# A four-block transformer-like network on one core: the high and low parts of x in one 512-column matmul in the gated feed-forwards

## The reference, cut to what matters

```python
D_MODEL, SEQ, D_FF = 1024, 256, 2816

def _rms_norm(x, g):
    y = x * lax.rsqrt(jnp.mean(x * x, axis=-1, keepdims=True) + 1e-6)
    return y * g

def _swiglu(x, w_gu, w_down):            # w_gu: 1024 x 5632, w_down: 2816 x 1024
    g, u = jnp.split(x @ w_gu, 2, axis=-1)
    return (jax.nn.silu(g) * u) @ w_down

# in each of the 4 layers, before and after the mixer:
x = x + 0.5 * _swiglu(_rms_norm(x, ffn_norm), w_gu, w_down)
```

## Time and profile before

| | us |
|---|---|
| median of 3 runs | 2880.78 (2880.45 to 2882.35) |
| profiled execution, its span (first to last instruction) | 2880.3 |
| TensorE matmul busy | 2797.6 (97%) |
| TensorE weight loads busy | 2594.2 (90%) |
| VectorE busy | 1953.6 (68%) |
| ScalarE busy | 1438.5 (50%) |
| HBM traffic | 478.46 MB, 166 GB/s |

### The profile page before, as it was taken

The page is one execution under the profiler, slowest core; times in us unless marked ns, Lnnn a source line. Parts: engine busy times, 40 slices in busy tenths (PEclk is TensorE's granted clock), DMA queues, the critical chain, the costliest instruction groups (busy, mean ns, idle before and its releaser), DMA issues.

```text
span 2880.3 us, 48145 instructions
## 1 busy us (share of the span) xinstructions
PE 2797.6 (97%) x20356; PEld 2594.2 (90%) x20356; DVE 1953.6 (68%) x2547; ACT 1438.5 (50%) x1970; POOL 94.6 (3%) x147
## 2 busy tenths in 40 slices
PE   8999989999999999999999999999899999999998
PEld 8999869999997999998889999988799989988997
DVE  5757876565666656556655565588755788767877
ACT  5445554444456444445544444456444644455543
POOL 0000000000012000001100000000000100000000
PEclk9999999999999999999999999999999999999999
DMA  7654336575552655553345555443465456544563
GB/s 245 205 162 146 125 113 202 184 211 188 163 163 73 213 190 177 189 176 93 108 140 188 176 190 185 153 147 111 140 196 184 152 176 211 179 161 139 174 215 102
DMA packets 406282, 478.46 MB, mean 166 GB/s; under 512 B 16634, under 2 KB 332820, under 8 KB 406068
## 3 DMA queue, kind: packets, MB, share of 16 engines
q1 hardware_dynamic: 404244, 469.07, 50.7%
q0 software_dynamic: 1632, 6.25, 0.8%
q10 hardware_dynamic: 192, 0.08, 0.0%
HBM read 474.29 MB, written 1.05 MB: 165 GB/s over the span
## 4 chain that ended last, share of the span: by engine, by line
PE 88%; DVE 7%; ACT 3%; issue 2%; POOL 0%; DMA 0%; ACTq 0%; POOLq 0%; DVEq 0%
PE Wk L710 18%; PE Wk L712 18%; PE Wk L711 18%; PE Y L710 10%; PE Y L711 9%; PE Y L712 9%; DVE w_lo L2006 2%; DVE work L2306 1%; PE Wk L1090 1%; PE Y L819 1%; ACT w_hi L1431 1%; PE Y L1103 1%; PE Y L1000 1%; PE Y L1074 0%; ACT work L1726 0%
## 5 line engine op out<-in xcount | busy, mean ns | idle before, releaser
L2006 DVE TENSOR_TENSOR w_lo<-ring,w_hi 128x1024 fp32r<-128x1024 f32 (+2 forms) x910 | 1068.2, 1199 | 561.6 <-ACT w_hi L1431 517.7
L710 PE MATMUL Wk<-xT_hi,w_hi 128*128 128x256 f32 x4320 | 1230.0, 285 | 7.5 <-DVE w_lo L2006 3.5
L712 PE MATMUL Wk<-xT_hi,w_lo 128*128 128x256 f32 x4320 | 1222.3, 283 | 0.0
L711 PE MATMUL Wk<-xT_lo,w_hi 128*128 128x256 f32 x4320 | 1222.2, 283 | 0.0
L1431 ACT ACTIVATE w_hi<-ring 128x1024 fp32r<-128x1024 f32 (+1 forms) x894 | 907.1, 1039 | 597.2 <-PE Wk L712 420.5
L710 PEld LDWEIGHTS Wk<-xT_hi,w_hi 128*128 128x128 f32 x4320 | 828.3, 192 | 18.7 <-issue 7.6
L711 PEld LDWEIGHTS Wk<-xT_lo,w_hi 128*128 128x128 f32 x4320 | 828.5, 192 | 4.7 <-issue 1.0
L712 PEld LDWEIGHTS Wk<-xT_hi,w_lo 128*128 128x128 f32 x4320 | 828.4, 192 | 0.0
L710 PE MATMUL Y<-w_hi,hid_hi 128*128 128x512 f32 x936 | 368.6, 394 | 5.0 <-issue 3.0
L711 PE MATMUL Y<-w_lo,hid_hi 128*128 128x512 f32 x936 | 365.8, 391 | 0.0
L712 PE MATMUL Y<-w_hi,hid_lo 128*128 128x512 f32 x936 | 364.4, 389 | 0.0
(11 more groups left out here) (308 smaller groups left out, 2661.0 us busy)
## 6 DMA issues: line engine op xcount, KB each, us to landing
ring<-in_ffn_w_gu SPq DMA_DIRECT2D x352, 512.0 KB, 4.4
ring<-in_ffn_w_down SPq DMA_DIRECT2D x224, 512.0 KB, 4.1
ring<-in_ffn_w_up SPq DMA_DIRECT2D x96, 512.0 KB, 6.3
ring<-in_hg_w_in SPq DMA_DIRECT2D x80, 512.0 KB, 3.6
ring<-in_na_w_in SPq DMA_DIRECT2D x24, 512.0 KB, 4.0
ring<-in_hg_w_out SPq DMA_DIRECT2D x16, 512.0 KB, 3.2
ring<-in_lru_w_in SPq DMA_DIRECT2D x16, 512.0 KB, 3.8
ring<-in_kv_w SPq DMA_DIRECT2D x16, 512.0 KB, 5.1
```

The lines of the kernel that those rows point to most:

```text
L710: pe.matmul(o, l_hi, r_hi, start=first, stop=False)
L711: pe.matmul(o, l_hi, r_lo, start=False, stop=False)
L712: return pe.matmul(o, l_lo, r_hi, start=False, stop=last)
L2006: ins = dve.tensor_tensor(l, r, h.bitcast(F32), ALU.subtract)
```

## The change: what it does

In the eight gated feed-forwards, and in them alone:

1. `xT_hi` and `xT_lo` become two halves of one tile, `xT_both`. The high weight block multiplies both at once, in one matmul of 512 columns (2 runs of 256, 2048 elements apart), into a bank of its own: the first 256 columns hold high by high, the other 256 high by low. The low weight block by high x, 256 columns, adds to the first half. Three matmuls become two. A product of one tile now takes two banks, one for each f: gate has banks 0 and 1, up has banks 2 and 3, for every chunk.
2. The two halves of a bank are added outside TensorE: ScalarE copies the second half of both banks (2 x 256 per partition) to `ff_rest`, VectorE adds it to the first half. This is done for gate and for up in each chunk.
3. As banks are no longer doubled over chunks, TensorE waits before the gate product for the scaled gate of the chunk before (`gate_scaled`), and before the up product for the hidden product of the chunk before (`hidden`).
4. The second multiplication by the root goes; the residual takes the token root `stat[:, 4 + tt]` in place of the number 0.5, and the hidden product takes a factor 0.5.
5. All feed-forwards take the late order of the last chunks, in the weight order, in TensorE's program and in ScalarE's wait before the last `hid_hi`.
6. VectorE waits for `r_ready` only before the first scaling of chunk 0, after the splits and after the addition; the saving of the small parameters moves from the end of chunk 2 to the middle of chunk 3.

```diff
-        xT_hi, xT_lo = sb("xT_hi", [P, KD, T], F32R), sb("xT_lo", [P, KD, T], F32R)
+        xT_both = sb("xT", [P, 2, KD, T], F32R)
+        xT_hi, xT_lo = xT_both[:, 0, :, :], xT_both[:, 1, :, :]
...
+        def halves_of(m, part):
+            return Wk[:, 2 * m:2 * m + 2, T * part:T * part + T]
...
             for j in range(1, chunks):
                 yield from gate_up(j)
-                if not (late and j == chunks - 2):
-                    if late and j == chunks - 1:
-                        yield from down_of(j - 2)
+                if j < chunks - 2:
                     yield from down_of(j - 1)
+            yield from down_of(chunks - 3)
+            yield from down_of(chunks - 2)
             yield from down_of(chunks - 1)
...
+            def two(o, l_hi, l_lo, r_both, first, last):
+
+                pe.matmul(o, l_hi, r_both, start=first, stop=False)
+                return pe.matmul(o[:, 0:T], l_lo, r_both[:, 0, :], start=False, stop=last)
+
             def f_part(u, o, f):
                 (t, h), (hi, lo) = u, split_of(u)
                 for i in range(4):
                     k, c = 4 * h + i, 256 * i + P * f
+                    if isinstance(o, tuple):
+                        mm = two(o[f], hi[:, c:c + P], lo[:, c:c + P], xT_both[:, :, k, :], k == 0, k == KD - 1)
+                        continue
                     mm = three(o[:, f * T:(f + 1) * T], ...)
...
+                in_halves = (bank(0), bank(1)), (bank(2), bank(3))
+                def gate_up(t, j):
+                    if not wide:
+                        f_product(t, bank(j % 2 * 2))
+                        f_product(t + 1, bank(j % 2 * 2 + 1))
+                        return
+                    pe.wait_ge(gate_scaled, f0 + j)
+                    f_product(t, in_halves[0])
+                    pe.wait_ge(hidden, n0 + j)
+                    f_product(t + 1, in_halves[1])
...
-                    gate_up(t0 + 3 * j - 1, j % 2)
-                    pe.wait_ge(hidden_ready, n0 + j)
-                    last_pair(s, a, b, lambda: pe.wait_ge(hidden_ready, n0 + j + 1))
+                gate_up(t0 + 3 * j - 4, j - 1)
+                pe.wait_ge(hidden_ready, n0 + j - 1)
+                gate_up(t0 + 3 * j - 2, j)
+                t_product(t0 + 3 * j, *hid(j - 2))
...
...
+                def rest_of(m, t):
+                    act.wait_ge(unit_done, units_to(t))
+                    act.activation(ff_rest[:, m, :, :], halves_of(m, 1), ACT.Copy).then_inc(rest_saved, 1)
+                def rest(j, h, g):
+                    rest_of(1, g + 2)
+                    hidden_hi(j, h, n0, free=end[s] - 3 if j == FF_CHUNKS - 1 else None)
+                ffn_stages(s, FF_CHUNKS, lambda j, h, g: rest_of(0, g + 1), gate, rest)
...
-                dve.wait_ge(r_ready, norms_before(s) + 1)
                 for j in range(FF_CHUNKS):
                     splits(g + 3)
-                    dve.wait_ge(unit_done, units_to(g + 1))
-                    dve.tensor_tensor(wide(ff_silu[:, h, :]), wide(bank(2 * h)), r_wide(2), ALU.mult)\
+                    dve.wait_ge(rest_saved, 2 * (f0 + j) + 1)
+                    step(dve.tensor_tensor(wide(ff_silu[:, h, :]), halves_of(0, 0), ff_rest[:, 0, :, :], ALU.add))
+                    if j == 0:
+                        dve.wait_ge(r_ready, norms_before(s) + 1)
+                    dve.tensor_tensor(wide(ff_silu[:, h, :]), wide(ff_silu[:, h, :]), r_wide(2), ALU.mult)\
                         .then_inc(gate_scaled, 1)
                     splits(g + 4)
+                    dve.wait_ge(rest_saved, 2 * (f0 + j) + 2)
+                    step(dve.tensor_tensor(wide(ff_hid[:, h, :]), halves_of(1, 0), ff_rest[:, 1, :, :], ALU.add))
                     dve.wait_ge(gate_act, n0 + j + 1)
-                    step(dve.tensor_tensor(wide(ff_silu[:, h, :]), wide(ff_silu[:, h, :]), r_wide(2), ALU.mult))
-                    dve.wait_ge(unit_done, units_to(g + 2))
-                    hidden_parts(j, h, n0, ff_silu[:, h, :], bank(2 * h + 1))
+                    hidden_parts(j, h, n0, ff_silu[:, h, :], ff_hid[:, h, :], 0.5)
...
+                c = stat[:, 4 + tt:5 + tt] if subs[s][0] == "ffn" else 1.0
                 dve.scalar_tensor_tensor(a, Y[:, 2 * tt + n, :], c, a, ALU.mult, ALU.add).then_inc(x_ready, 1)
```

More of the change, by code:

```diff
@@ L447, in t_src, with ffn_tiles @@
             return w[r0:r0 + 256, :].rearrange("(k p) n -> p k n", p=P)
-        def ffn_tiles(gu, down, chunks, F, late=False):
+        def ffn_tiles(gu, down, chunks, F):
             def gate_up(j):
@@ L471, in chunk_at @@
             first = base[s] + 3 * j - (j > 0)
-            return first - 1 if subs[s][0] == "cffn" and j == chunks - 1 else first
+            return first - 1 if j == chunks - 1 else first
         def tiles_of(kind, idx, layer):
@@ L885, in ffn @@
                 t0 = base[s]
[L886 to L890, removed]
+                n0, f0 = before(s, {"ffn": FF_CHUNKS, "cffn": CF_CHUNKS}), before(s, {"ffn": FF_CHUNKS})
+                wide = has_norm(s)
+                in_halves = (bank(0), bank(1)), (bank(2), bank(3))
[8 more added lines that the diff above has]
+                    f_product(t + 1, in_halves[1])
                 def hid(j):
                     return (a[:, j % 2, :].rearrange("p (k t) -> p k t", k=2) for a in (hid_hi, hid_lo))
-                enter(s, (bank(0), bank(1)))
-                late = by_tokens(s)
-                for j in range(1, chunks - 1 - late):
-                    gate_up(t0 + 3 * j - 1, j % 2)
+                enter(s, in_halves if wide else (bank(0), bank(1)))
+                for j in range(1, chunks - 2):
+                    gate_up(t0 + 3 * j - 1, j)
                     pe.wait_ge(hidden_ready, n0 + j)
                     if s == 0 and j == PARAMETERS_AT:
+                        pe.wait_ge(gate_scaled, f0 + j + 1)
                         first_parameters()
@@ L906, in ffn @@
                 a, b = (t0 + 3 * j + 1, *hid(j - 1)), (t0 + 3 * j + 2, *hid(j))
[L907 to L911, removed]
+                gate_up(t0 + 3 * j - 4, j - 1)
+                pe.wait_ge(hidden_ready, n0 + j - 1)
+                gate_up(t0 + 3 * j - 2, j)
+                t_product(t0 + 3 * j, *hid(j - 2))
+                if by_tokens(s):
                     last_by_tokens(s, [a, b], [lambda: pe.wait_ge(hidden_ready, n0 + j),
@@ L1510, in save_r, with ffn_stages @@
                 act.activation(r_row[:, :], bank(6)[:, 0:T], ACT.Copy).then_inc(r_ready, 1)
-            def ffn_stages(s, chunks, gate, rest):
+            def ffn_stages(s, chunks, first, gate, rest):
                 for j in range(chunks):
@@ L1517, in ffn_stages @@
                     splits(g + 3)
+                    first(j, j % 2, g)
                     if j == 0 and has_norm(s):
@@ L1560, in rest @@
                     hidden_hi(j, h, n0, free=end[s] - 3 if j == CF_CHUNKS - 1 else None)
-                ffn_stages(s, CF_CHUNKS, both, rest)
+                ffn_stages(s, CF_CHUNKS, lambda j, h, g: None, both, rest)
             def sigmoid(z, done):
@@ L2772, in _ @@
                 else:
-                    residual(s, 0.5 if kind == "ffn" else 1.0)
+                    residual(s)
 def constants():
```

33 lines of the change are left out of this document (17 added, 16 removed).

## The result

The changed kernel takes 2862.68 us in the median of 4 runs (2860.24 to 2864.58) against 2881.49 for the kernel before on the same chip: 18.8 us less, ratio 0.9935 with a 95% interval of 0.9921 to 0.9948. Faster, as forecast, but by half of the 38 us, and outside the range of 2837 to 2858. The profiled execution spans 2860.6 us where the sum had 2842.0.

A forecast was written before the change was run, and what follows sets the result against it. TensorE's matmuls were taken as the bound (97% of the span, 88% of the chain of waits). 2880.3 - 36 (pairs) - 3.8 (mixer entries) + 1.5 (first entry) = 2842.0 profiled, so 2843 us; range 2837 to 2858.

The forecast's parts named there:

- The pair of matmuls: Gate and up products: a pair falls from 0.360 to 0.348 us; over 2816 pairs, 36 us off the path.
- rival C: The 0.012 us belongs to weight loads a 256-column stream doesn't hide; half the gain given back, 18 us: 2861, chance 0.03.
- Rival A: Covers run short: seven more entries lose 1.5 us each, eight ends 0.5 each, 14 us: 2857, chance 0.12.
- Rival B: The wide matmul's second run of moving operand costs like a matmul start; no gain on pairs: 2879, chance 0.04.
- The Trainium skill's 2.5 ns: Alternative fixed part per matmul, from the skill's page: 7 us gain on the pairs in place of 36; not adopted.
- VectorE and ScalarE hide their work: Per chunk: 61 us more VectorE and 104 more ScalarE busy time in all, nothing on the path; waits covered by 7 us.
- rival D: Without a second accumulator buffer TensorE waits in every chunk; 1.23 us exposed a chunk is 108 us: 2951, chance 0.04.
- Entries after a mixer: After the two HGRN2 mixers, splits ahead of the root wait let TensorE start 1.9 us earlier each: 3.8 us gone.
- The first entry: First sublayer: addition and scaling end at 26.1 while TensorE's covering unit ends at 24.65; 1.5 us lost.
- Ends: Feed-forward ends in the late order, four low parts before the residual: nothing, at worst 0.5 us in each of 8.

The follow-up runs named there:

- x_unmerged: Changed kernel with the wide matmul split again, three matmuls of 256 columns a pair, all else as changed: 2881.27 us, ratio 0.9999 to the kernel before.
- x_group8: Changed kernel with each unit's 8 wide matmuls issued in a row, then its 8 narrow ones (4 and 4 in a sublayer's first tiles): 2849.9 us.
- m_loads: TensorE alone, no network, weight blocks of 128, 96, 64, 32 columns: 512 and 256 in turn took 352.6, 351.7, 340.8, 348.0 ns a pair; same block repeated 347.1.
- x_contig: Changed kernel with high and low x side by side, so the wide matmul reads one run of 512 columns instead of two of 256: 2863.1 us.
- x_rootfirst: Changed kernel, but VectorE waits for the saved root before any split of a feed-forward, as the kernel before did: 2905.6 us.
- x_entry0: Changed kernel; in the first sublayer VectorE waits for POOL's diagonals, splits two units, adds and scales the first gate, then splits the others: 2859.03 us.
- m_widths: TensorE alone, no network, matmul streams of uniform, alternating and grouped widths: 512 and 256 in turn 353.3 ns a pair, groups of 8 349.2.

## Why the prediction was wrong, step by step

- **The pair of matmuls: mis-sized, and this is the step that failed.** The step "one of 512 and one of 256 columns, 0.228 + 0.120 = 0.348" took the distances of uniform streams for an alternation. The pair costs 0.3528. What went on the pairs is 2816 x 0.007 = 19 to 20 us, not 36. The down product behind them, which the prediction left at 5.47, costs 0.03 more in each chunk, 3 us. By the chunks (16.98 to 16.79) the merging is worth some 17 us; x_unmerged against the changed kernel gives 18. That is 19 us short of the 36. x_group8 shows that it is the order of the widths: the same matmuls in groups give 13 of them back.
- **What the trace of before had shown of it.** The surplus sat in the first matmuls behind each narrow stream:

```profile
621.75 0.40 PE L710 MATMUL Y<-w_hi,hid_hi 128*128 128x512 f32 x1
621.99 0.40 PE L711 MATMUL Y<-w_lo,hid_hi 128*128 128x512 f32 x1
622.22 0.39 PE L712 MATMUL Y<-w_hi,hid_lo 128*128 128x512 f32 x1
622.45 0.40 PE L710 MATMUL Y<-w_hi,hid_hi 128*128 128x512 f32 x1
```

In nanoseconds the first two distances are 234 and 236 where the stream settles at 227, and the first narrow one behind wide ones is 113 where it settles at 120: switches were to be seen, once per chunk, and the change makes 32 of them there. Against rival C the text looked at the last matmul before each switch, which does keep its distance (120 and 227); the effect stands behind the switch, and dividing by 24 spread it into the 0.228.
- **Rival C** (half of the fixed part given back, 2861) came within 2 us of the measured time, at a chance of 0.03. The half was an estimate without a row, so the closeness is in part luck. Its claim that the fixed part isn't wholly given back fits; its cause, the weight load, is not shown: m_loads went neither way.
- **Rival A** (seven entries and all ends run short, 2857): not borne out. One more entry lost 0.6 us, and no end did.
- **Rival B** (two runs): refuted by x_contig, which had them in one run.
- **The Trainium skill's 2.5 ns** (TensorE: Matmul & The Clock Gate, Back-to-back issue gap), which that page gives for a matmul by itself, is not the fixed part of these streams: uniform ones stand at 13.3 ns over the columns at 512, 384, 320 and 256, and at 11.7 at 288. The prediction adds that by the page weight loads come on top in a stream; the page says so of few columns only, and for 512 it has streams at some 131 ns, below its formula, where they stand at 227 here. Going by the rows was right.
- **VectorE and ScalarE hide their work: right.** 16.79 us a chunk without a wait; x_unmerged shows the cost as nothing. The chain was 2.3 us as worked out, and rival D's wait in every chunk did not come.
- **Entries after a mixer: right**, 2 x 1.9 us. What the order would cost in the new frame, had it been left, was not asked: x_rootfirst shows 43 us.
- **The first entry: wrong in mechanism.** Forecast: 1.5 us, for `gate_scaled`. It was POOL's diagonals beside VectorE's splits, which came 3.2 us later, and 2.4 us of low clock behind it: 5.6. The third feed-forward lost 0.6 us in the same way. The step moved VectorE's splits past a wait and looked only at who waits for VectorE, not at who works beside it. x_entry0 gives 3.7 of it back.
- **Ends: right.** No wait stood in the transposes beyond the 0.7 us that both kernels have.
- **What stays open.** The corrected terms, -17 for the chunks, -3.8, +5.6 and +0.6, come to 14 or 15 us of gain where 18.8 were measured and 19.7 stand between the two profiled executions. The mixers, in which no step of the prediction expected a change, were together 4.5 us shorter in the changed kernel's execution (each from the root's small matmuls at its entry to those of the next sublayer), the latent attention (1.8) and the second HGRN2 mixer (2.3) above all. Between executions of the other kernels of this document these two stages differ by 2 to 3 us as well. So part of the gain came from stages for which no run shows a reason, and the sum would have missed by 4 to 5 us more without it.

## What to carry to other kernels

A mean distance between matmuls belongs to the order it was read in. Before merging matmuls of one size into a mix of two, read the distances right behind each change of size, in nanoseconds. If they differ, time a few group sizes on TensorE alone and issue the sizes in the best one: here grouping the same matmuls gave another 13 us of the 19 that the merging had missed, and the cost did not fall evenly with the size of the group.

When an in-order engine is set free earlier, look also at the engine beside it: work that was quick while the other waited may slow down and be late. And a wait can cost more than its length: here TensorE stood for 3.4 us and then ran 8 pairs at its lower clock, 2.4 us more.

## What the runs showed of the hardware

- float32r streams with a new 128-column weight block each cost their columns at 2.4 GHz and 13.3 ns, at 256, 320, 384 and 512 columns (m_widths); at 288 it was 11.7 ns.
- Mixing widths costs beside that: 512 in turn with 256, 320 and 384 gave 6.6, 6.6 and 12.6 ns a pair; in groups of 8 and 16 it was some 26 ns over the first five wide ones and 7 ns back on the first narrow one, in groups of two only 4 ns there and back (m_widths). For 512 with 256 it was the same with one or two runs of the moving operand, one or two banks, and with VectorE and ScalarE at work or still; it did shift with the number of weight columns (m_loads).
- A `tensor_scalar` of 128x128 on POOL took 0.6 us with VectorE idle, 1.2 with a split of VectorE over its first 0.7 us (the kernel before), and 2.2 to 2.4 beside splits nearly all along (the changed kernel).
- After standing for 3.4 us TensorE ran its next 8 pairs at the lower clock (the changed kernel), and after five waits of 3.7 to 3.8 us 5 to 10 wide matmuls each (x_rootfirst); a pair took 0.64 us there.
